# RMSNorm statistics by quarter, down-projection groups of 3 and 4, and norms moved across two stage barriers in a decoder layer

## The chip, the cores and the metric

The kernel runs on the 8 cores of one Trainium2 chip. Each core computes 2 of the 16 sequences from beginning to end; nothing is exchanged. The metric is the device time in microseconds of the slowest core.

## The reference

One decoder layer on x of 16 × 2048 × 1024 float32, and a last norm. In short:

```
x = x + 0.5 * swiglu(rmsnorm(x, g1), gate1, up1, down1)      # D = 1024, D_FF = 2816
h = rmsnorm(x, g_mix)
proj = h @ w_in                                              # 1024 -> 3072
A = 4 differential-attention heads (causal, over all 2048 keys)
B = 8 dilated sliding-window heads, windows/strides (128,1), (512,4), (2048,16)
x = x + concat(A, B) @ w_out
x = x + 0.5 * swiglu(rmsnorm(x, g2), gate2, up2, down2)
y = rmsnorm(x, g_fin)
rmsnorm(x, g) = x / sqrt(mean(x*x) + 1e-5) * g ; swiglu = (silu(x@gate) * (x@up)) @ down
```

## The kernel before, in words

A sequence is held in SBUF as `x_sb`: 16 tiles (NT) of 128 tokens by 1024 features, float32. Its stages run one after the other, for each of the two sequences: FFN1 norm, FFN1, mix norm, differential attention and its output projection, dilated attention and its output projection, FFN2 norm, FFN2, final norm.

A norm that feeds matmuls is `norm_to_hT` (L344). It loads the gain (one transfer on SyncE's queue, L336), calls `row_stats_all` (L338), and then goes over the 16 tiles. `row_stats_all` is 16 Square activations on ScalarE (L297; each squares a tile into `junk` and adds up its rows into a column of `ss`), one Sqrt over all 16 columns, and one reciprocal on VectorE (L342) that leaves `rstd`. For each tile VectorE multiplies by `rstd` and gain into one of two buffers `hb` (L308), TensorE transposes its eight 128×128 blocks into PSUM bank 6 or 7 (L353), and the bank is copied into `hT`, by ScalarE for even tiles (L356) and by VectorE for odd ones (L315). `final_norm` (L762) has no transposes: VectorE writes the tile into one of two output buffers (in `acc`) and SyncE's queue sends it to HBM.

`ffn` (L361) goes over 22 chunks of 128 hidden features. Per chunk and quarter of the tokens: 8 gate and 8 up matmuls of 128×512 (PSUM banks 0 to 3), Silu on ScalarE, a product on VectorE into a ring `aT` of 8 chunks. The weights of a chunk are three transfers that GpSimd issues, into rings of 3 (gate, up) and 6 (down) chunks. After every fourth chunk, and after the last, comes a down-projection group: for 16 tiles and 2 halves, one matmul per chunk of the group is summed up in PSUM bank 4 or 5, and VectorE adds 0.5 times the bank to `x_sb` (L308, `scalar_tensor_tensor`). So the groups have 4, 4, 4, 4, 4 and 2 chunks.

The order on each engine is the order of emission; nothing is reordered. `Sched.op` (L74) derives the waits from declared reads and writes. `Sched.barrier` (L64) notes the last operation of every engine and the last DMA of every semaphore key; the next operation that each engine has after it waits for them all, and `run_engine` (L149) writes that as one wait instruction after the other, leaving out those that this engine has made before:

```
            for d in o.deps:
                sem, val = d.signal
                k = id(sem)
                if waited.get(k, 0) < val:
                    eng.wait_ge(sem, val)
```

A barrier stands after FFN1, after the mix norm, after the first output projection, and after the second one. Behind the mix norm's barrier SyncE loads the positions, VectorE and ScalarE compute rotation tables in turn (`rope_tables`, each step waits for the one before), and GpSimd issues four `w_out` loads and then the first `w_in` loads. SBUF region `U16` is shared: the FFN's weight rings lie where the attention's `mixT`, which the output projection reads, lies.

Of the kernel before, what the change touches and what calls it, by code (L numbers as in the profile page):

```python
# [14 lines left out]
D = 1024  # L15
# [5 lines left out]
G = 4  # L21
LAMBDA_INIT = 0.8 - 0.6 * math.exp(-0.3 * 0)
# [145 lines left out]
def build_nc(nseq=2, stages=("ffn1", "attn", "ffn2"), debug_out=None):  # L168
# [88 lines left out]
    R_ss = Res("ss")  # L257
    R_rstd = Res("rstd")
# [79 lines left out]
    def row_stats_all():  # L338
        for t in range(NT):
            act(junk[:], x_sb[:, t, :], AF.Square, [R_x[t]], [R_junk, R_ss], accum_out=ss[:, t:t + 1])  # L340
        act(rstd[:], ss[:], AF.Sqrt, [R_ss, R_eps], [R_rstd], bias=epsc[:], scale=1.0 / D)
        SC.op("dve", lambda e: e.reciprocal(out=rstd[:], in_=rstd[:]), [R_rstd], [R_rstd])  # L342

    def norm_to_hT(g_ap):  # L344
        load_gain(g_ap)
        row_stats_all()
        for t in range(NT):
            k = t % 2
            stt("dve", hb[:, k, :], x_sb[:, t, :], rstd[:, t:t + 1], gain[:], ALU.mult, ALU.mult,
                [R_x[t], R_rstd, R_gain], [R_hb[k]])  # L350
            for dc in range(8):
                SC.op("pe", lambda e, o=pt[k][:, dc * 128:(dc + 1) * 128], i=hb[:, k, dc * 128:(dc + 1) * 128]:
                      e.transpose(o, i, ident[:]), [R_hb[k], R_ident], [R_pt[k]])  # L353
            src = pt[k].rearrange("p (c t) -> p c t", c=8)
            if t % 2 == 0:
                SC.op("act", lambda e, o=hT[:, :, t * 128:(t + 1) * 128], i=src: e.copy(out=o, in_=i),  # L356
                      [R_pt[k]], [R_hT[t]])
            else:
                tcopy("dve", hT[:, :, t * 128:(t + 1) * 128], src, [R_pt[k]], [R_hT[t]])

    def ffn(wg_d, wu_d, wd_d):  # L361
# [4 lines left out]
        for c in range(NCH):  # L366
# [18 lines left out]
            if (c + 1) % G == 0 or c == NCH - 1:  # L385
                c0 = (c // G) * G
                grp = list(range(c0, c + 1))
# [361 lines left out]
    def attention(s_, which):  # L749
        norm_to_hT(g_mix)  # L750
# [6 lines left out]
        if "B" in which:  # L757
            dil_stage()
            out_proj(512)
        SC.barrier()  # L760

    def final_norm(s):  # L762
        load_gain(g_fin)
        row_stats_all()
        for t in range(NT):
            k = t % 2
            stt("dve", ostage[:, k, :], x_sb[:, t, :], rstd[:, t:t + 1], gain[:], ALU.mult, ALU.mult,
                [R_x[t], R_rstd, R_gain], [R_ostage[k]])
# [3 lines left out]
    for s in range(nseq):  # L772
        for t in range(NT):
            dma("sp", x_sb[:, t, :], x_in[s, t * 128:(t + 1) * 128, :], [], [R_x[t]], ("x", t))
        if "ffn1" in stages:
            norm_to_hT(g_ffn1)
            ffn(w1g, w1u, w1d)
            SC.barrier()
# [6 lines left out]
        if "ffn2" in stages:  # L785
            norm_to_hT(g_ffn2)
# [88 lines left out]
```

How the kernel before makes its waits and increments, by code:

```python
    def run_engine(self, e, eng, final_waits=None):  # L149
        waited = {}
        for o in self.ops[e]:
            for d in o.deps:
                sem, val = d.signal
                k = id(sem)
                if waited.get(k, 0) < val:
                    eng.wait_ge(sem, val)
                    waited[k] = val
            ins = o.fn(eng)
            if o.need_inc:
                sem, _ = o.signal
                ins.then_inc(sem, 16 if o.dma_key is not None else 1)
        if final_waits:
            for sem, val in final_waits:
                if waited.get(id(sem), 0) < val:
                    eng.wait_ge(sem, val)
```

## Time and profile before

| what | value |
|---|---|
| time of three runs: lowest, median, highest | 4325.0, 4445.0, 4617.3 us |
| time of the profiled execution | 4323.8 us |
| its span (first to last instruction, slowest core) | 4322.2 us |
| spans of the eight cores | 4305.7 to 4322.2 us |
| TensorE matmul busy | 3355.8 us, 15640 matmuls |
| VectorE busy / ScalarE busy / GpSimd busy | 1717.8 / 1283.3 / 677.2 us |

The profiled execution is one run, and lies next to the lowest of the three; the times of single instructions below come from it. Its own time is 1.6 us more than its span. "Busy" of TensorE is the time in which matmuls were under way. In rows of a timeline the first number is the start in us from the span's start, the second the duration; a bracket tells how long the engine had been idle before, and what ended that. "issue" there means that the engine waited for nothing that the profile shows. The times are of core 5.

### The profile page before, as it was taken

The numbers are of one execution on the slowest core, as the hardware profiler recorded it, in microseconds if no ns is written. First come the engines' busy times: TensorE is split into PE (matmuls) and PEld (weight loads), VectorE is DVE, ScalarE is ACT, GpSimd is POOL, SyncE is SP. The second block draws the span as 40 slices with busy tenths as digits, with TensorE's granted clock in tenths as the row PEclk, the third lists the DMA queues.
The fourth block names the chain that finished last, engine by engine and source line by source line (L and its number), as shares of the span: only waits on it lengthen the run. The fifth ranks groups of instructions, "written<-read, shape, count | busy, mean of one in ns | idle before, by whom it ended". The sixth has DMA issues, their size and how long they took to land.

```text
span 4322.2 us, 57072 instructions; the slowest of 8 cores (4305.7 to 4322.2 us)
## 1 busy us (share of the span) xinstructions
PE 3355.8 (78%) x15640; PEld 1404.4 (32%) x15640; DVE 1717.8 (40%) x2611; ACT 1283.3 (30%) x1959; POOL 677.2 (16%) x904
## 2 busy tenths in 40 slices
PE   1999955777587767999739999468776787599995
PEld 1444322232133323344214434132322333244442
DVE  2333444131355454433533343441314454543345
ACT  2111022636344542011221101236362546311102
POOL 0111002120043320011001100020201343101100
PEclk9999977888676668999959999678887675699998
DMA  4333202010111013233243322110101010223321
GB/s 107 37 40 40 25 6 35 1 16 1 15 11 11 6 22 37 32 38 41 46 144 42 42 30 25 20 20 1 16 1 20 6 16 1 27 35 38 44 30 78
DMA packets 256900, 129.76 MB, mean 30 GB/s; under 512 B 228816, under 2 KB 233040, under 8 KB 256592
## 3 DMA queue, kind: packets, MB, share of 16 engines
q0 software_dynamic: 243776, 86.00, 18.2%
q1 hardware_dynamic: 12816, 40.11, 2.7%
q8 instruction: 137, 2.24, 0.2%
q14 instruction: 171, 1.40, 0.1%
HBM read 195.30 MB, written 16.78 MB: 49 GB/s over the span
## 4 chain that ended last, share of the span: by engine, by line
PE 70%; issue 7%; DVE 7%; ACT 7%; DMA 6%; POOL 1%; SPq 0%; DVEq 0%; ACTq 0%; POOLq 0%
PE pall L290 65%; DMA U<-w_in 4%; PE pall L714 3%; PE pall L353 2%; ACT tmpf L295 2%; ACT U L295 2%; ACT junk L297 2%; DVE hb L308 1%; POOL U L312 1%; DVE x_sb L308 1%; DVE tmpf L312 1%; DMA y<-acc 1%; DVE acc L312 1%; DVE U L312 1%; DMA x_sb<-x 1%
## 5 line engine op out<-in xcount | busy, mean ns | idle before, releaser
L290 PE MATMUL pall<-hT,U 128*128 128x512 bf16 x6912 | 1543.7, 384 | 104.7 <-DMA U<-w_in 68.9
L290 PE MATMUL pall<-U 128*128 128x512 bf16 (+5 forms) x5424 | 1358.5, 383 | 224.5 <-DVE tmpf L312 99.1
L290 PEld LDWEIGHTS pall<-hT,U 128*128 128x128 bf16 x6912 | 680.4, 99 | 944.7 <-issue 153.6
L290 PEld LDWEIGHTS pall<-U 128*128 128x128 bf16 (+1 forms) x5424 | 429.5, 101 | 1108.9 <-issue 873.0
L295 ACT ACTIVATE tmpf<-pall 128x512 f32<-128x512 f32 (+1 forms) x384 | 243.0, 633 | 1623.3 <-PE pall L290 1623.2
L312 DVE TENSOR_TENSOR U<-tmpf,pall 128x512 bf16<-128x512 f32 x352 | 242.1, 688 | 978.8 <-PE pall L290 961.1
L308 DVE SCALAR_TENSOR_TENSOR x_sb<-pall,x_sb 128x512 f32<-128x512 f32 x768 | 529.7, 692 | 196.9 <-PE pall L290 195.4
L295 ACT ACTIVATE U<-pall 128x1024 bf16<-128x1024 f32 (+5 forms) x688 | 463.4, 697 | 299.4 <-PE pall L290 289.0
L312 DVE TENSOR_TENSOR U<-U,maskb 128x256 bf16<-128x256 bf16 (+1 forms) x496 | 143.0, 303 | 672.9 <-ACT U L295 672.0
L312 POOL TENSOR_TENSOR U<-U,maskb 128x256 bf16<-128x256 bf16 (+1 forms) x448 | 253.8, 571 | 910.9 <-ACT U L295 557.7
L353 PE MATMUL pall<-ident,hb 128*128 128x128 bf16 x768 | 96.5, 306 | 350.1 <-DVE hb L308 288.9
L290 PE MATMUL pall<-U,onesb 128*128 128x512 bf16 (+3 forms) x672 | 263.3, 400 | 71.3 <-ACT U L295 71.3
L286 POOL DMA_DIRECT2D U<-ffn_gate x88 | 78.4, 891 | 1318.4 <-PE pall L290 1221.5
L714 PE MATMUL pall<-U 128*128 128x128 bf16 (+1 forms) x816 | 189.2, 345 | 82.9 <-POOL U L312 52.7
L312 POOL TENSOR_TENSOR U<-tmpf 128x512 bf16<-128x512 f32 x128 | 170.8, 1351 | 183.2 <-DVE tmpf L312 144.3
L297 ACT ACTIVATE junk<-x_sb 128x1024 bf16<-128x1024 f32 x128 | 135.2, 1056 | 214.9 <-DVE x_sb L312 75.4
L353 PEld LDWEIGHTS pall<-ident,hb 128*128 128x128 bf16 x768 | 74.5, 138 | 373.0 <-issue 372.7
L312 DVE TENSOR_TENSOR tmpf<-junk,U 128x512 f32<-128x512 bf16 x128 | 135.9, 1062 | 106.8 <-POOL U L312 62.7
L480 ACT CAST junk<-pall 128x512 bf16<-128x512 f32 x128 | 74.8, 586 | 312.4 <-PE pall L290 255.1
L312 DVE TENSOR_TENSOR acc<-pall,acc 128x512 f32<-128x512 f32 x128 | 129.3, 1063 | 0.2 <-PE pall L714 0.2
L286 POOL DMA_DIRECT2D U<-ffn_down x88 | 49.5, 563 | 496.7 <-PE pall L290 496.7
L714 PEld LDWEIGHTS pall<-U 128*128 128x128 bf16 x816 | 62.1, 113 | 196.6 <-issue 195.3
(53 smaller groups left out, 1449.9 us busy)
## 6 DMA issues: line engine op xcount, KB each, us to landing
U<-ffn_gate POOLq DMA_DIRECT2D x88, 256.0 KB, 4.4
U<-ffn_up POOLq DMA_DIRECT2D x88, 256.0 KB, 6.3
U<-ffn_down POOLq DMA_DIRECT2D x88, 256.0 KB, 6.7
x_sb<-x SPq DMA_DIRECT2D x32, 512.0 KB, 13.2
y<-acc SPq DMA_DIRECT2D x32, 512.0 KB, 2.8
U<-w_in POOLq DMA_DIRECT2D x40, 256.0 KB, 4.5
U<-w_out POOLq DMA_DIRECT2D x16, 256.0 KB, 6.6
tmpf<-ffn_norm SPq DMA_DIRECT2D x4, 512.0 KB, 13.2
```

The lines of the kernel that those rows point to most:

```text
L286: return SC.op(eng, lambda e, o=out, i=in_: e.dma_start(out=o, in_=i), reads, writes, dma_key=key)
L290: e.matmul(o, lhsT=l, rhs=r, start=s, stop=t), reads, writes)
L295: e.activation(out=o, in_=i, func=f, bias=b, scale=s), reads, writes)
L297: e.activation(out=o, in_=i, func=f, bias=b, scale=s, accum_out=a), reads, writes)
L308: e.scalar_tensor_tensor(out=o, in0=i, scalar=s, in1=j, op0=p, op1=q), reads, writes)
L312: e.tensor_tensor(out=o, in0=i, in1=j, op=p), reads, writes)
L353: e.transpose(o, i, ident[:]), [R_hb[k], R_ident], [R_pt[k]])
L480: SC.op("act", lambda e, o=qraw[:, k, :], i=A[:]: e.copy(out=o, in_=i), [R_pb[k]], [R_qraw[k]])
L714: e.matmul(o, lhsT=l, rhs=r, start=s_, stop=False, skip_group_check=True),
```

## The change

The statistics are computed for four tiles at a time, each quarter with its own Sqrt and reciprocal over four columns, and each quarter is emitted inside the tile loop, ahead of its first tile; `ss` and `rstd` have a resource per quarter, so that a tile waits for its own quarter alone. The table `GROUP_END` sets the down groups to chunks 0–2, 3–5, 6–9, 10–13, 14–17, 18–21. The barrier between FFN1 and the mix norm is gone. The FFN2 norm is emitted ahead of the barrier that follows the second output projection, so that this barrier now stands between the FFN2 norm and FFN2.

```diff
+GROUP_END = {2: 0, 5: 3, 9: 6, 13: 10, 17: 14, 21: 18}
...
-    R_ss = Res("ss")
-    R_rstd = Res("rstd")
+    R_ss = [Res(f"ss{q}") for q in range(4)]
+    R_rstd = [Res(f"rstd{q}") for q in range(4)]
...
-    def row_stats_all():
-        for t in range(NT):
-            act(junk[:], x_sb[:, t, :], AF.Square, [R_x[t]], [R_junk, R_ss], accum_out=ss[:, t:t + 1])
-        act(rstd[:], ss[:], AF.Sqrt, [R_ss, R_eps], [R_rstd], bias=epsc[:], scale=1.0 / D)
-        SC.op("dve", lambda e: e.reciprocal(out=rstd[:], in_=rstd[:]), [R_rstd], [R_rstd])
+    def row_stats(q):
+        sl = slice(4 * q, 4 * q + 4)
+        for t in range(4 * q, 4 * q + 4):
+            act(junk[:], x_sb[:, t, :], AF.Square, [R_x[t]], [R_junk, R_ss[q]], accum_out=ss[:, t:t + 1])
+        act(rstd[:, sl], ss[:, sl], AF.Sqrt, [R_ss[q], R_eps], [R_rstd[q]], bias=epsc[:], scale=1.0 / D)
+        SC.op("dve", lambda e: e.reciprocal(out=rstd[:, sl], in_=rstd[:, sl]), [R_rstd[q]], [R_rstd[q]])
 
     def norm_to_hT(g_ap):
         load_gain(g_ap)
-        row_stats_all()
         for t in range(NT):
             k = t % 2
+            if t % 4 == 0:
+                row_stats(t // 4)
             stt("dve", hb[:, k, :], x_sb[:, t, :], rstd[:, t:t + 1], gain[:], ALU.mult, ALU.mult,
-                [R_x[t], R_rstd, R_gain], [R_hb[k]])
+                [R_x[t], R_rstd[t // 4], R_gain], [R_hb[k]])
...
-            if (c + 1) % G == 0 or c == NCH - 1:
-                c0 = (c // G) * G
-                grp = list(range(c0, c + 1))
+            if c in GROUP_END:
+                grp = list(range(GROUP_END[c], c + 1))
...
     def attention(s_, which):
-        norm_to_hT(g_mix)
         SC.barrier()
         rope_tables(s_)
...
             dil_stage()
             out_proj(512)
+        if "ffn2" in stages:
+            norm_to_hT(g_ffn2)
         SC.barrier()
 
     def final_norm(s):
         load_gain(g_fin)
-        row_stats_all()
         for t in range(NT):
             k = t % 2
+            if t % 4 == 0:
+                row_stats(t // 4)
...
         if "ffn1" in stages:
             norm_to_hT(g_ffn1)
             ffn(w1g, w1u, w1d)
-            SC.barrier()
+        if any(st in stages for st in ("attn", "attnA", "attnB")):
+            norm_to_hT(g_mix)
...
         if "ffn2" in stages:
-            norm_to_hT(g_ffn2)
+            if not any(st in stages for st in ("attn", "attnA", "attnB")):
+                norm_to_hT(g_ffn2)
             ffn(w2g, w2u, w2d)
```

ScalarE's queue, from the first norm to the mix norm, stands like this in the kernel before (`junk,ss<-x_sb` are the Squares, `rstd<-ss` the Sqrt, `COPY hT` the copies of the even tiles, `tmpf<-pall` the FFN's Silu):

```order
L297 ACTIVATE junk,ss<-x_sb 128x1024 x16
L295 ACTIVATE rstd<-ss,epsc 128x16
L356 COPY hT<-pall 128x8x128 x8
L295 ACTIVATE tmpf<-pall 128x512 x88
L297 ACTIVATE junk,ss<-x_sb 128x1024 x16
L295 ACTIVATE rstd<-ss,epsc 128x16
L356 COPY hT<-pall 128x8x128 x8
```

and like this in the changed kernel, over the first norm:

```order
L298 ACTIVATE junk,ss<-x_sb 128x1024 x4
L296 ACTIVATE rstd<-ss,epsc 128x4
L359 COPY hT<-pall 128x8x128 x2
L298 ACTIVATE junk,ss<-x_sb 128x1024 x4
L296 ACTIVATE rstd<-ss,epsc 128x4
L359 COPY hT<-pall 128x8x128 x2
L298 ACTIVATE junk,ss<-x_sb 128x1024 x4
L296 ACTIVATE rstd<-ss,epsc 128x4
L359 COPY hT<-pall 128x8x128 x2
L298 ACTIVATE junk,ss<-x_sb 128x1024 x4
L296 ACTIVATE rstd<-ss,epsc 128x4
L359 COPY hT<-pall 128x8x128 x2
```

The 16 Squares in one piece have become four pieces of four; from the second piece on they stand behind two copies of the quarter before.

SyncE's queue from the first gain load to the FFN2 norm's, with its waits (`s_` are the engines' semaphores, `d_` those of DMA keys; `tmpf` is the gain, `acc` the positions), before:

```order
L286 DMA tmpf<-ffn_norm 128x1024
L286 DMA tmpf<-mix_norm 128x1024 [waits d_25,s_dve,s_pe,s_act,d_35,d_26,d_27,d_28,d_29,d_30,d_31,d_32,d_33,d_34,d_36,d_37,d_0,d_3,d_7,d_8,d_9,d_10,d_11,d_12,d_13,d_14,d_15,d_16,d_17,d_18,d_19,d_20,d_21,d_22,d_23,d_24]
L286 DMA acc<-positions 128x512 [waits s_pe,s_act,s_dve,d_25]
L286 DMA acc<-positions 128x512
L286 DMA acc<-positions 128x512 [waits d_38,s_dve]
L286 DMA acc<-positions 128x512 [waits d_39,s_dve]
L286 DMA tmpf<-ffn_norm 128x1024 [waits s_pe,s_act,s_dve,s_pool,d_39,d_40,d_41,d_42,d_43,d_44,d_45,d_38]
```

and changed:

```order
L287 DMA tmpf<-ffn_norm 128x1024
L287 DMA tmpf<-mix_norm 128x1024 [waits d_25,s_dve]
L287 DMA acc<-positions 128x512 [waits s_pe,s_act,s_dve,d_35,d_25,d_26,d_27,d_28,d_29,d_30,d_31,d_32,d_33,d_34,d_36,d_37,d_0,d_3,d_7,d_8,d_9,d_10,d_11,d_12,d_13,d_14,d_15,d_16,d_17,d_18,d_19,d_20,d_21,d_22,d_23,d_24]
L287 DMA acc<-positions 128x512
L287 DMA acc<-positions 128x512 [waits d_38,s_dve]
L287 DMA acc<-positions 128x512 [waits d_39,s_dve]
L287 DMA tmpf<-ffn_norm 128x1024 [waits s_pe,s_act,s_dve,s_pool,d_39,d_40,d_41,d_42,d_43,d_44,d_45,d_38]
```

The long list of waits has moved from the mix norm's gain load to the first load of positions, since that is now SyncE's first operation behind the first barrier. The same happens on VectorE (from the mix norm's reciprocal to the first step of the rotation tables) and on ScalarE (from the mix norm's first Square to the first Sin of the tables).

## Rows read from the trace of the kernel before

**Rows 1.** Busy by stretch: PE, PEld, DVE, ACT, POOL (counts), clock, DMA share, GB/s.

```profile
1603.00:1660.00 57.00, 16.53 (x130) 12.73 (x131) 24.54 (x25) 28.07 (x42) 6.99 (x9) 0.52 0.43 53
```

**Rows 2.** Timeline, FFN1 end and mix norm, sequence 0: start, duration (us), engine, what.

```profile
592.36 0.69 DVE L308 SCALAR_TENSOR_TENSOR x_sb<-pall,x_sb 128x512 f32<-128x512 f32 x1 [0.25 <-PE pall L290]
...
594.36 1.06 ACT L297 ACTIVATE junk<-x_sb 128x1024 bf16<-128x1024 f32 x1 [28.01 <-issue]
...
595.17 0.33 SPq L286 DMA_DIRECT2D tmpf<-mix_norm  x1
...
612.96 1.06 ACT L297 ACTIVATE junk<-x_sb 128x1024 bf16<-128x1024 f32 x1
...
615.48 0.31 ACT L295 ACTIVATE rstd<-ss,epsc 128x16 f32<-128x16 f32 x1
...
617.12 0.25 DVE L342 RECIPROCAL rstd<-rstd 128x16 f32<-128x16 f32 x1 [24.07 <-issue]
...
654.18 0.69 DVE L315 COPY hT<-pall 128x1024 bf16<-128x1024 bf16 x1 [1.26 <-PE pall L353]
```

**Rows 3.** Timeline, second output projection's end, FFN2 norm, FFN2's start, sequence 0.

```profile
1601.99 0.69 DVE L312 TENSOR_TENSOR x_sb<-pall,x_sb 128x512 f32<-128x512 f32 x1 [0.41 <-PE pall L290]
...
1603.60 0.94 POOL L286 DMA_DIRECT2D U<-ffn_gate  x1 [48.18 <-DVE x_sb L312]
...
1625.17 0.25 DVE L342 RECIPROCAL rstd<-rstd 128x16 f32<-128x16 f32 x1 [22.49 <-ACT rstd L295]
...
1632.58 1.01 ACT L356 COPY hT<-pall 128x1024 bf16<-128x1024 bf16 x1 [3.33 <-PE pall L353]
...
1634.29 2.47 DVE L308 SCALAR_TENSOR_TENSOR hb<-x_sb,rstd,tmpf 128x1024 bf16<-128x1024 f32 x2
...
1659.44 10.88 PE L290 MATMUL pall<-hT,U 128*128 128x512 bf16 x42
...
1659.75 0.69 DVE L315 COPY hT<-pall 128x1024 bf16<-128x1024 bf16 x1 [1.26 <-PE pall L353]
```

**Rows 4.** Timeline, first norm of sequence 0: gain transfer's issue, first normalization.

```profile
47.34 4.06 SPq L286 DMA_DIRECT2D tmpf<-ffn_norm  x1
...
70.36 2.48 DVE L308 SCALAR_TENSOR_TENSOR hb<-x_sb,rstd,tmpf 128x1024 bf16<-128x1024 f32 x2 [0.17 <-DVE rstd L342]
```

**Rows 5.** DMA issues of 40 to 70 us, gain row: KB, us from issue to landing.

```profile
tmpf<-ffn_norm SPq DMA_DIRECT2D x1, 512.0 KB, 20.7
```

**Rows 6.** DMA issues, first gate weights at 118.0, 3740.9 and 1603.6 us.

```profile
U<-ffn_gate POOLq DMA_DIRECT2D x1, 256.0 KB, 4.6
...
U<-ffn_gate POOLq DMA_DIRECT2D x1, 256.0 KB, 6.7
...
U<-ffn_gate POOLq DMA_DIRECT2D x1, 256.0 KB, 9.5
```

**Rows 7.** Timeline, VectorE adds of a two-chunk group, then of a four-chunk group.

```profile
570.49 1.36 DVE L308 SCALAR_TENSOR_TENSOR x_sb<-pall,x_sb 128x512 f32<-128x512 f32 x2 [0.17 <-PE pall L290]
...
588.94 1.36 DVE L308 SCALAR_TENSOR_TENSOR x_sb<-pall,x_sb 128x512 f32<-128x512 f32 x2 [0.17 <-PE pall L290]
...
1719.46 0.69 DVE L308 SCALAR_TENSOR_TENSOR x_sb<-pall,x_sb 128x512 f32<-128x512 f32 x1 [0.41 <-PE pall L290]
...
1747.02 0.69 DVE L308 SCALAR_TENSOR_TENSOR x_sb<-pall,x_sb 128x512 f32<-128x512 f32 x1 [0.41 <-PE pall L290]
```

**Rows 8.** Timeline, final norm of sequence 0: last add, first output tile.

```profile
2146.44 0.69 DVE L308 SCALAR_TENSOR_TENSOR x_sb<-pall,x_sb 128x512 f32<-128x512 f32 x1 [0.17 <-PE pall L290]
...
2150.65 2.48 DVE L308 SCALAR_TENSOR_TENSOR acc<-x_sb,rstd,tmpf 128x1024 f32<-128x1024 f32 x2 [0.18 <-DVE rstd L342]
```

**Rows 9.** Groups by line, ScalarE's table loads: busy us, mean ns, idle before.

```profile
L295 ACT ACT_TABLE_LOAD x16 | 20.5, 1283 | 65.5 <-DVE lams L327 34.8 <-DVE tmpf L304 17.7 <-PE pall L290 12.3
```

**Rows 10.** Timeline, after mix norm: positions' issue, first rotation matmul.

```profile
655.01 4.47 SPq L286 DMA_DIRECT2D acc<-positions  x3
...
688.59 0.58 PE L290 MATMUL pall<-junk,perm 128*128 128x512 bf16 x1 [10.29 <-ACT junk L480]
```

More of the change, by code:

```diff
@@ L763, in final_norm @@
         load_gain(g_fin)
-        row_stats_all()
         for t in range(NT):
             k = t % 2
+            if t % 4 == 0:
+                row_stats(t // 4)
             stt("dve", ostage[:, k, :], x_sb[:, t, :], rstd[:, t:t + 1], gain[:], ALU.mult, ALU.mult,
-                [R_x[t], R_rstd, R_gain], [R_ostage[k]])
+                [R_x[t], R_rstd[t // 4], R_gain], [R_ostage[k]])
             out_dmas.append(dma("sp", y_out[s, t * 128:(t + 1) * 128, :], ostage[:, k, :], [R_ostage[k]], [],
```

## The prediction

> **What bounds the kernel now.** I read the busy time by stretch first, then the timeline of the norms, the adds of the down groups, the transfers and the table loads. TensorE is busy for 78% of the span, so what can be won lies where it is not, and the norms are such places. In the FFN2 norm of sequence 0 it works 16.5 of 57 us, VectorE 24.5 and ScalarE 28.1 [rows 1]: no engine is the bound, they take turns. The reader is to see two halves there. First 16 Squares in a row, one every (612.96 − 594.36)/15 = 1.24 us, then Sqrt and reciprocal [rows 2]. Then the tile loop, from the reciprocal at 1625.17 to the end of the last copy at 1660.44, 35.3 us [rows 3], in which VectorE multiplies two tiles, waits for the transposes and copies one. Whatever of a norm lies beside a matmul stage is won; whatever is moved inside the tile loop is not hidden, since TensorE's next matmuls stand behind the transposes of all 16 tiles.
>
> **The statistics inside the loop.** This is the term that decides. In the changed order ScalarE has 4 Squares, Sqrt, 2 copies, 4 Squares and so on. The Squares of quarter 1 stand behind the copy of tile 2, and that copy waits for tile 2's transposes. In the loop of before this copy ends at 1632.58 + 1.01 = 1633.59, and VectorE starts tile 4 at 1634.29 [rows 3]. Now 4 Squares (4 × 1.24 = 4.96), the Sqrt (0.31, [rows 2]) and the reciprocal (0.25, [rows 3]) come in between, with three handovers of about 0.2 (the reciprocal's to the multiply is 0.17, [rows 4]): tile 4 starts at about 1633.59 + 5.86 = 1639.45, 5.2 us late. That comes three times per norm, 15.5 us; the Squares of quarter 0 alone can be ahead of the loop. So a loop costs 35.3 + 15.5 = 50.8 us from its first reciprocal. At least the 4.96 us of Squares less the 0.7 of slack, 4.3, must show; 6.0 would need half a microsecond for each handover: 13 to 18 us per norm.
>
> **FFN1 norm.** The Squares were hidden before: they follow x from HBM. Now only quarter 0 is needed early, but the first multiply also needs the gain, which SyncE issues behind all 16 tiles of x, at 47.34, and which lands 20.7 us later, at 68.0 [rows 4, 5]. Before, the first multiply started at 70.36 [rows 4]. So it comes at 68.2, 2.2 us sooner, and the loop is 15.5 longer: **+13.3 us**. Were the gain there at once, tile 0 could start some 17 us sooner, but it is not, and the change leaves its place in the queue alone.
>
> **Mix norm.** Before, from the last add's end (592.36 + 0.69 = 593.05) to the last copy's end (654.87) it is 61.8 us [rows 2]. Now the Squares of quarter 0 run under the last down group, the gain has long landed, and VectorE's reciprocal stands right behind its last add: 0.1 + 50.8 = 50.9, so 10.9 less. But the barrier's waits were paid in this stretch: ScalarE's first Square came 1.3 us after the last add, SyncE's gain load 2.1, and the reciprocal started 617.12 − 615.79 = 1.3 after the Sqrt [rows 2]. These lists are not removed but move to the first operation behind the mix norm, as the order of SyncE's queue shows: the load of positions, which came 0.14 us after the last copy (655.01, [rows 10]), then VectorE's first table step, then ScalarE's first Sin. These are one chain, and TensorE waits at its end: 10.3 us for a cast that stands behind the last Sin [rows 10]. So 2.0 + 1.2 + 1.2 = 4.4 come back. TensorE's and GpSimd's own lists are covered by that wait. **−6.5 us** (−10.9 if the lists cost nothing there).
>
> **FFN2 norm.** The last add of the output projection ends at 1602.68, FFN2's first matmul comes at 1659.44 [rows 3]. Now the loop's last copy ends at 1602.68 + 0.1 + 50.8 = 1653.6. But the barrier has moved behind it, and with it the first weights, which before were issued at 1603.60 under the Squares, 0.9 us after the barrier's last operation [rows 3]: issue at 1654.5, landing 4.6 to 9.5 us later. I take the middle row, 6.7 [rows 6]; the shortest is of the steady state with no burst of nine loads, the longest had the gain load beside it. TensorE's own list of ten waits adds about 0.8, priced like GpSimd's 0.9. First matmul at 1662.0: **+2.6 us** (+0.5 to +5.4). Here the cover that hid the loads is gone, and it eats the 5.9 us that the hidden quarter wins.
>
> **Final norm.** The Squares already ran beside the last down group; from the last add's end (2147.13) to the first output tile it took 3.5 us: a Square, a table load, Sqrt, reciprocal [rows 8]. Now quarter 0 is done long before, and reciprocal and handovers remain, 0.5 us. The later quarters' reciprocals fall into VectorE's waits for the output buffers. **−3.0 us**.
>
> **Down groups.** Work is the same: 22 × 32 matmuls and 6 × 32 adds per FFN. A group is paced by its two PSUM banks, which are filled, read and refilled in turn: a pair of adds takes (588.94 − 570.49)/12 = 1.54 us with two chunks and (1747.02 − 1719.46)/14 = 1.97 with four [rows 7]. That is 0.216 per matmul of each bank's sum, so three chunks should take 1.755. Then before 5 × 16 × 1.97 + 16 × 1.54 = 182.2 us per FFN, after 4 × 16 × 1.97 + 2 × 16 × 1.755 = 182.2. **0 us**. The bounds are three chunks at the pace of two (2 × 16 × 0.215 = −6.9 per FFN, −28 over four) or of four (+28). The weights' ring of six down chunks frees its slots as early as before: groups end at 2, 5, 9, 13, 17 and the load of chunk c needs c − 6 done, never later than chunk c − 3.
>
> **Table loads.** The Trainium skill, "ScalarE: Activation LUTs", section "Table sets: the hidden batching unit", says to batch activations by table set, and speaks against Sqrts strewn among other functions; it names copy among the fillers of every set, but not the Square. By that rule each switch would cost what its section "What ACT_TABLE_LOAD costs" gives, about 2.66 us with its drain; an estimate from this page is 2 × 3 × 6 switches, some 96 us. What follows does not need the page. The trace has 16 loads of 1.28 us [rows 9]. Counting the changes of function in the program (Exp at the start; Sqrt, Silu, Sqrt, Sin, Exp with Ln, Sqrt, Silu, Sqrt in sequence 0; in sequence 1 the same less the first Sqrt) gives 1 + 8 + 7 = 16, so no Square and no copy ever brought one, and the new Sqrts bring none. By this count the term is 0.
>
> **Sum.** Per sequence 13.3 − 6.5 + 2.6 − 3.0 = +6.4; I take both sequences alike, so +12.8 us: 4323.8 + 12.8 = 4336.6, **4337 us**, +0.3%. This stands against the profiled execution, at the low end of the three runs. Their median is 4445, 2.8% above it, more than all terms together; the same program can come out there again (4445 + 13 = 4458).
>
> **Rivals.**
> - *The statistics overlap as meant.* If ScalarE's Squares of later quarters cost the loop nothing, 6 × 15.5 = 93 us go: 4244. The order speaks against it: in a queue that runs in order they stand behind copies that wait. 3%.
> - *Three-chunk groups run at the pace of VectorE.* Two chunks at 1.54 are near two adds of 0.69 with their handovers; if three are too, −28: 4309. Against it: two matmuls more per bank already cost their full time between two and four chunks. 12%.
> - *Three-chunk groups at four chunks' pace*, +28: 4365. 5%.
> - *Slower: table reloads.* If the Square or the copy needed another set than Sqrt, each of three later quarters in six norms would load twice on the path: 36 × 1.28 = 46 us, 4383. It decides from the first load seen between a copy and a Square. The count above is against it. 4%.
> - *Slower: the weights behind the moved barrier.* If gate weights land after 9.5 us and the stall per quarter is 6.0, it is 2 × 2.8 + 6 × 2.5 = +21: 4358. 8%.
>
> **How the numbers follow.** The forecast (4337) has 65%, the rivals 32%, something not thought of 3%. The terms' own bounds give 4315 to 4358; the low end 4300 takes in the case of faster three-chunk groups; the high end 4460 takes in the slower cases and a run at the median shown before. All cases lie within 2% (86 us), about what a measurement of this kernel can tell from no change; for a scatter like that of the runs shown, and for what I missed, I leave 7% faster and 7% slower, 86% within.
>
> **What would show it.** In the changed profile: 16 table loads again; in each tile loop three gaps of VectorE of about 5 us before tiles 4, 8 and 12, ended by ScalarE; last add to last copy about 51 us at the mix norm; the positions' load 2 us after the mix norm; FFN2's first matmul waiting for its gate weights, some 8 us after the last copy; first output tile 0.5 us after the last add; a pair of adds at 1.75 us in the groups of three. It is wrong if the Squares of later quarters lie beside the copies of earlier ones, if more than 16 table loads are there, or if an FFN's length changed by more than a few us.

## The result and the profile after

The changed kernel takes 4394.7 us, the median of 10 runs (4347.82 to 4761.62); the kernel before, run beside it, 4426.2 (10 runs, 4324.18 to 4709.0). Some executions of either kernel run with the TensorE clock of one die lower and take 80 to 410 us longer, 6 of the 10 of before and 5 of the 10 of the changed kernel, which is why the medians stand the other way round; so the two are compared without them, and so is every ratio below. That ratio is **1.0066 (95% interval 1.005 to 1.0082)**: the change costs 0.7% or about 28 us. The forecast was 12.8 us. The profiled execution took 4350.43 us against 4323.8. First two of its cores:

```profile
core 1: 4348.9 us, clock 0.843
core 5: 4346.6 us, clock 0.844
```

One core of each die, at the clock that before had on them (0.844 and 0.845): the difference is work and waits, not clock.

**Where it went.** From the timelines of all eight cores of both kernels I took the times of a few events of VectorE (the last add and the last copy of a norm, the first product of an FFN, the first and last output tile) and of the output projections' ends. The table has the mean of eight cores of each stage, in us, as sequence 0 / sequence 1. A norm between two stages is the same on all cores to within 0.5. The stages that wait for transfers (the first norm of a sequence, attention, FFN2's first weights, the output tiles of sequence 0) differ by up to 6 from the shortest to the longest core, so that a mean of eight is good to about 1.

| stage | before | after | measured | forecast |
|---|---|---|---|---|
| start (sequence 1: last output tile of sequence 0) to the last copy of the FFN1 norm | 104.7 / 67.9 | 117.9 / 81.1 | +13.2 / +13.2 | +13.3 |
| FFN1, last copy to last add | 487.9 / 486.2 | 486.3 / 487.2 | −1.6 / +1.0 | 0 |
| mix norm, last add to last copy | 61.8 / 60.7 | 49.3 / 49.7 | −12.6 / −11.1 | −10.9 |
| to the end of the first output projection | 512.1 / 509.6 | 516.9 / 514.7 | +4.8 / +5.0 | +4.4 |
| to the end of the second | 431.8 / 430.0 | 433.4 / 432.2 | +1.6 / +2.2 | 0 |
| FFN2 norm and wait for its first product | 62.2 / 62.2 | 65.2 / 64.7 | +3.0 / +2.5 | +2.6 |
| FFN2, first product to last add | 481.9 / 481.6 | 481.0 / 480.7 | −0.9 / −0.9 | 0 |
| last add to first output tile | 3.5 / 3.5 | 0.3 / 0.3 | −3.2 / −3.2 | −3.0 |
| first to last output tile | 32.2 / 31.7 | 42.3 / 33.3 | **+10.1** / +1.7 | 0 |
| sum | 4311.4 | 4336.2 | +24.8 | +12.8 |

All terms that were forecast with a size came within 2 us. What was missed stands in rows forecast as 0: the output tiles (+11.8) and the way to the second output projection (+3.8); the FFNs give 2.4 back.

**The tile loop.** These rows are VectorE's and ScalarE's part of the mix norm in the timeline of after, sequence 0, core 1 ([rows 2] has that of before):

```profile
603.31 0.69 DVE L309 SCALAR_TENSOR_TENSOR x_sb<-pall,x_sb 128x512 f32<-128x512 f32 x1 [0.18 <-PE pall L291]
603.92 0.17 DVE L344 RECIPROCAL rstd<-rstd 128x4 f32<-128x4 f32 x1
...
610.85 1.01 ACT L359 COPY hT<-pall 128x1024 bf16<-128x1024 bf16 x1 [3.43 <-PE pall L356]
611.76 1.06 ACT L298 ACTIVATE junk<-x_sb 128x1024 bf16<-128x1024 f32 x1
...
617.12 0.18 DVE L344 RECIPROCAL rstd<-rstd 128x4 f32<-128x4 f32 x1 [4.47 <-ACT rstd L296]
617.40 2.48 DVE L309 SCALAR_TENSOR_TENSOR hb<-x_sb,rstd,tmpf 128x1024 bf16<-128x1024 f32 x2
...
630.65 0.18 DVE L344 RECIPROCAL rstd<-rstd 128x4 f32<-128x4 f32 x1 [4.47 <-ACT rstd L296]
...
644.19 0.18 DVE L344 RECIPROCAL rstd<-rstd 128x4 f32<-128x4 f32 x1 [4.48 <-ACT rstd L296]
...
652.56 0.69 DVE L316 COPY hT<-pall 128x1024 bf16<-128x1024 bf16 x1 [1.26 <-PE pall L356]
```

Read it from ScalarE's side: its copy of tile 2 (610.85) has to wait for tile 2's transposes, and the four Squares of the next quarter stand right behind it, so VectorE has nothing to multiply for 4.47 us. The first reciprocal, on the other hand, stands right behind the last add (603.31 + 0.69 = 604.00; the trace has the reciprocal start 0.08 before that). Last add to last copy is 653.25 − 604.00 = 49.3 us where 50.9 was forecast.

**The FFN2 norm's end**, timeline of after, sequence 0, core 1, and its gate transfer in the view of DMA issues (KB, us to landing):

```profile
1654.51 0.69 DVE L316 COPY hT<-pall 128x1024 bf16<-128x1024 bf16 x1 [1.27 <-PE pall L356]
1655.64 0.33 SPq L287 DMA_DIRECT2D tmpf<-final_norm  x1
1656.17 0.94 POOL L287 DMA_DIRECT2D U<-ffn_gate  x1 [97.67 <-DVE hT L316]
...
1664.41 15.87 PE L291 MATMUL pall<-hT,U 128*128 128x512 bf16 x62 [10.00 <-DMA U<-ffn_gate]
```

```profile
U<-ffn_gate POOLq DMA_DIRECT2D x1, 256.0 KB, 7.8
```

TensorE stands for 10.0 us, and it names the gate weights. They are issued 1.0 us after the last copy's end and land 7.8 us later; before, they were issued 0.9 us behind the output projection's last add, ahead of the norm [rows 3]. Compare [rows 1] with the same norm in after on the same core, 5 (PE, PEld, DVE, ACT, POOL busy with counts, clock, DMA share, GB/s). TensorE and VectorE work about as long as before. ScalarE has 5.6 us less, the Squares and the Sqrt of quarter 0. GpSimd's 6.99 us, the issues of the weights, are gone from the norm, and no transfer is under way in it. No engine is the bound in after either.

```profile
1603.50:1654.00 50.50, 16.18 (x128) 12.39 (x128) 25.79 (x29) 22.46 (x35) 0.00 (x0) 0.52 0.00 0
```

**The first norm**, after, core 1. The reciprocal of quarter 0 comes at 49.59, some 20 us before that of before, which stood right ahead of the multiply at 70.36 [rows 4]. Yet this wins only 1.6 and 2.2 us (mean of the cores, sequence 0 and 1), since the multiply now waits for the gain. The second fence is ScalarE's table loads in the view of groups: 16 again, as in [rows 9].

```profile
46.70 4.28 SPq L287 DMA_DIRECT2D tmpf<-ffn_norm  x1
...
49.59 0.18 DVE L344 RECIPROCAL rstd<-rstd 128x4 f32<-128x4 f32 x1 [10.23 <-ACT rstd L296]
68.25 2.48 DVE L309 SCALAR_TENSOR_TENSOR hb<-x_sb,rstd,tmpf 128x1024 bf16<-128x1024 f32 x2 [18.48 <-DMA tmpf<-ffn_norm]
```

```profile
L296 ACT ACT_TABLE_LOAD x16 | 20.5, 1283 | 98.3 <-PE pall L291 35.4 <-DVE lams L328 35.1 <-DVE tmpf L305 14.2
```

**The output tiles of sequence 0**, where most of the missed time is. First comes the timeline of after (core 1), then the transfers issued in this stretch, then the same two of before (core 5):

```profile
2151.28 0.55 POOL L287 DMA_DIRECT2D U<-ffn_down  x1 [29.73 <-PE pall L291]
...
2151.95 0.88 POOL L287 DMA_DIRECT2D U<-ffn_gate  x1
...
2152.44 2.48 DVE L309 SCALAR_TENSOR_TENSOR acc<-x_sb,rstd,tmpf 128x1024 f32<-128x1024 f32 x2 [0.18 <-DVE rstd L344]
...
2155.97 0.60 POOL L287 DMA_DIRECT2D U<-ffn_down  x1
2163.06 2.48 DVE L309 SCALAR_TENSOR_TENSOR acc<-x_sb,rstd,tmpf 128x1024 f32<-128x1024 f32 x2 [8.15 <-DMA y<-acc]
...
2173.13 2.50 DVE L309 SCALAR_TENSOR_TENSOR acc<-x_sb,rstd,tmpf 128x1024 f32<-128x1024 f32 x2 [7.50 <-DMA y<-acc]
```

```profile
y<-acc SPq DMA_DIRECT2D x6, 512.0 KB, 8.6
U<-ffn_down POOLq DMA_DIRECT2D x3, 256.0 KB, 11.8
U<-ffn_gate POOLq DMA_DIRECT2D x2, 256.0 KB, 10.5
```

```profile
2120.28 0.88 POOL L286 DMA_DIRECT2D U<-ffn_gate  x1 [69.53 <-PE pall L290]
...
2126.58 0.93 POOL L286 DMA_DIRECT2D U<-ffn_up  x1
2146.68 0.56 POOL L286 DMA_DIRECT2D U<-ffn_down  x1 [19.17 <-PE pall L290]
...
2154.86 2.50 DVE L308 SCALAR_TENSOR_TENSOR acc<-x_sb,rstd,tmpf 128x1024 f32<-128x1024 f32 x2 [1.73 <-DMA y<-acc]
```

```profile
y<-acc SPq DMA_DIRECT2D x12, 512.0 KB, 2.7
```

Look at GpSimd first (in after there are three down, two gate and two up loads in this stretch). The next sequence's loads (gate, up, down of chunk 0 and so on) stand in its queue in order. A ring slot holds every sixth chunk, so the down load of chunk 0 takes slot 0, in which chunk 18 of this sequence lies. Before, the last group was 20 and 21, chunk 18 was used up in the group 16 to 19, and eight loads went out at 2120 to 2127, under the matmuls; only that of chunk 2 waited. Now the last group is 18 to 21. The load of chunk 0 waits 29.73 us for its end, six more stand behind it, and all seven meet the first output stores. A store then takes 8.6 us instead of 2.7, and VectorE has only two output buffers: it waits twice for about 8 us instead of 1.7.

**The wait lists**, core 5 after, behind the mix norm. The last copy is issued at 652.80; against [rows 10] the positions' load, the first table step and the Sin's table load are all late:

```profile
652.80 0.69 DVE L316 COPY hT<-pall 128x1024 bf16<-128x1024 bf16 x1 [1.26 <-PE pall L356]
655.70 17.42 SPq L287 DMA_DIRECT2D acc<-positions  x4
...
662.98 0.49 DVE L303 TENSOR_SCALAR tmpf<-acc,invf 128x512 f32<-128x512 int32 x1 [9.48 <-issue]
...
668.00 1.28 ACT L296 ACT_TABLE_LOAD   x1 [15.29 <-issue]
```

From the last copy's end (653.49) the three are 2.2, 9.5 and 14.5 us; before they were 0.1, 3.7 and 7.7. Not all of this is lists: on this core the positions also took 5.9 us to land, and 3.4 before, and over cores and sequences that time scatters from 3.1 to 6.7 before and from 3.5 to 6.0 in after. What is the same on all eight cores of sequence 0 is 2.1 us more ahead of the issue, and a first table step 1.4 us behind the landing instead of 0.17; from that step to the table load it is 5.0 us instead of 3.9 to 4.3. The first rotation matmul, at the end of this chain, comes 39.8 and 38.0 us after the last copy (sequence 0 and 1, mean of the cores), and came 34.3 and 34.5 before. The profile writes "issue" for a list, since no semaphore event ends it.

### The profile page after: what moved, and what is told of

The parts are those of the page before. It is cut to its first block, busy times and chain, and to the rows that moved or that the text cites. A ratio compares the mean times of both kernels' runs of the same rounds, so it can differ in the third digit from the quotient of the medians.

```text
span 4348.9 us, 57066 instructions; the slowest of 8 cores (4330.5 to 4348.9 us)
## 1 busy us (share of the span) xinstructions
PE 3368.6 (77%) x15640; PEld 1404.9 (32%) x15640; DVE 1718.6 (40%) x2635; ACT 1288.3 (30%) x1983; POOL 678.4 (16%) x904
## 4 chain that ended last, share of the span: by engine, by line
PE 71%; issue 8%; DMA 7%; DVE 6%; ACT 6%; POOL 1%; SPq 0%; DVEq 0%; ACTq 0%; POOLq 0%
PE pall L291 65%; DMA U<-w_in 3%; PE pall L716 3%; ACT tmpf L296 2%; ACT U L296 2%; PE pall L356 2%; DVE hb L309 2%; ACT junk L298 1%; POOL U L313 1%; DMA y<-acc 1%; DVE tmpf L313 1%; DMA tmpf<-ffn_norm 1%; DVE U L313 1%; DVE acc L313 1%; PE pall L664 1%
## 5 line engine op out<-in xcount | busy, mean ns | idle before, releaser
L309 DVE SCALAR_TENSOR_TENSOR hb<-x_sb,rstd,tmpf 128x1024 bf16<-128x1024 f32 x96 | 118.8, 1279 | 38.7 <-DMA tmpf<-ffn_norm 36.1
L359 ACT COPY hT<-pall 128x1024 bf16<-128x1024 bf16 x48 | 48.6, 1012 | 270.3 <-PE pall L356 270.3
## 6 DMA issues: line engine op xcount, KB each, us to landing
tmpf<-ffn_norm SPq DMA_DIRECT2D x4, 512.0 KB, 12.1
```

Source lines behind the costliest of these rows:

```text
L309: e.scalar_tensor_tensor(out=o, in0=i, scalar=s, in1=j, op0=p, op1=q), reads, writes)
```

## The experiments

The ratios are against the kernel before, run on the same chip. "Stages" are means of eight cores, worked out as in the table above; where a stage is named without a sequence, sequence 0 stands first.

**Groups back.** The changed kernel with the old groups:

```diff
-GROUP_END = {2: 0, 5: 3, 9: 6, 13: 10, 17: 14, 21: 18}
+GROUP_END = {3: 0, 7: 4, 11: 8, 15: 12, 19: 16, 21: 20}
```

> The changed kernel with the down groups of before (4,4,4,4,4,2 chunks). Theory, burst of weights: with chunk 18 in the last group, the next sequence's first down load waits for that group's end, and six gate, up and down loads behind it in GpSimd's queue are issued together with the first output tiles; these took 8.6 us to land instead of 2.7. With the old groups the burst is over before the outputs begin: from the first to the last output tile of sequence 0 the time falls from 42.3 (mean of the cores) to about 33 us, the other stages stay, and the span falls by 9 to 12 us, to about 4338. Rival, pace of the groups: the groups of three and four themselves cost the time; then the two FFNs of a sequence get shorter or longer by several us, and the output stretch stays at 42.

Measured: 1.0035 (1.002 to 1.005), profiled 4341.14 us. The output tiles of sequence 0 are back at 33.2 us (after 42.3), and a store lands after 2.8 us. The four FFNs, in their order, move by +1.3, 0.0, −0.8 and +1.7 against after. So the regrouping costs through the output tiles, and not in the FFNs (what these 0.8 to 1.7 us are stands in the last section).

**Groups only.** The kernel before with the new groups and nothing else:

```diff
+GROUP_END = {2: 0, 5: 3, 9: 6, 13: 10, 17: 14, 21: 18}
-            if (c + 1) % G == 0 or c == NCH - 1:
-                c0 = (c // G) * G
-                grp = list(range(c0, c + 1))
+            if c in GROUP_END:
+                grp = list(range(GROUP_END[c], c + 1))
```

> The kernel before with the new group table alone. Theory, burst of weights: the output stretch of sequence 0 grows from 32.2 to 38 to 44 us (the first output tile comes 3.5 us later here than in the changed kernel, so some of the burst is past), all else stays, span 4322 + 6 to 12 = 4328 to 4334. Rival, pace of the groups: FFN stages change by more than 2 us each and the output stretch stays near 32. Nothing at all (4322) would say that the burst needs the other edits.

Measured: 1.0036 (1.0018 to 1.0053). Sequence 0's output tiles take 39.7 us against 32.2, +7.5, and those of sequence 1 +0.1: the cost needs a next sequence whose weights are to be loaded. The rest of the +15.7 us of the sum lies in the attention (+1.0, −0.3, +4.3, +0.4), in FFN2 of sequence 0 (+1.6) and FFN1 of sequence 1 (+1.1; see the last section). The +4.3, on the way to the first output projection of sequence 1, is more than the scatter of a mean, and no edit of this run touches that stage: its cause is open, and it is a warning for what small differences of this stage are taken to show. By the ratios both experiments give about the same: half of what the change costs is the regrouping.

**Groups 3, 4, 4, 4, 4, 3.** A last group of three, 19 to 21, so that chunk 18 is done one group earlier:

```diff
-GROUP_END = {2: 0, 5: 3, 9: 6, 13: 10, 17: 14, 21: 18}
+GROUP_END = {2: 0, 6: 3, 10: 7, 14: 11, 18: 15, 21: 19}
```

> The changed kernel with groups of 3, 4, 4, 4, 4 and 3 chunks, so that the last group holds chunks 19 to 21 and no longer chunk 18, whose slot the next sequence's first down load takes. Theory, burst of weights: the slot decides, not the sizes: the output stretch of sequence 0 falls from 42.3 to about 33 us as in the run with the old groups, FFN stages stay within 1 us, span about 4339. Rival, any last group of three or four chunks delays the outputs (its adds end later beside them): stays at 40 or above.

Measured: 4345.37 us in the profiled run; there is no ratio for it. The output tiles take 38.4 us, so 4.0 of 9.1 us are gone, where I had expected all of them to go. The timeline of its slowest core has the reason, and it is the same mechanism:

```profile
2158.05 0.56 POOL L287 DMA_DIRECT2D U<-ffn_down  x1 [24.20 <-PE pall L291]
2158.72 0.88 POOL L287 DMA_DIRECT2D U<-ffn_gate  x1
...
2168.97 2.66 DVE L309 SCALAR_TENSOR_TENSOR acc<-x_sb,rstd,tmpf 128x1024 f32<-128x1024 f32 x2 [7.50 <-DMA y<-acc]
2173.15 2.58 DVE L309 SCALAR_TENSOR_TENSOR acc<-x_sb,rstd,tmpf 128x1024 f32<-128x1024 f32 x2 [1.44 <-DMA y<-acc]
```

Now it is the load of chunk 1 that waits, for chunk 19, and three loads are behind it instead of six. VectorE waits once for 7.5 us instead of twice. What the stores lose goes by how many loads come out at the group's end: one, four, seven loads give 33.2, 38.4, 42.3 us.

**Statistics first.** The changed kernel, but with the Squares and Sqrts of all four quarters ahead of the loop; only the reciprocals stay at the quarters:

```diff
+        for q in range(4):
+            row_stats(q)
...
-                row_stats(t // 4)
+                row_recip(t // 4)
```

> The changed kernel with the Squares and Sqrts of all four quarters emitted ahead of the tile loop in the six norms with transposes; the reciprocals stay at each quarter. Theory, order of ScalarE's queue: the three stalls of about 4.9 us in each loop are the Squares behind the copies; they go, and at the mix and FFN2 norms the Squares lie beside the adds before them. Norm from last add to last copy 49.4 to about 36 us, FFN1 norm's loop 49.7 to about 36, six times 13.5 = 81 us less: span about 4268. Rival, cost per quarter: the stall comes with each quarter's own Sqrt, reciprocal and waits wherever the Squares are; then loops stay above 45 us and the span above 4325.

Measured: **0.987 (0.9848 to 0.9893)**, profiled 4265.31 us, 83 us less than after in the stages' sum. The loop's rows (mix norm, sequence 0, slowest core):

```profile
597.25 0.17 DVE L347 RECIPROCAL rstd<-rstd 128x4 f32<-128x4 f32 x1
597.52 2.48 DVE L309 SCALAR_TENSOR_TENSOR hb<-x_sb,rstd,tmpf 128x1024 bf16<-128x1024 f32 x2
...
606.22 0.17 DVE L347 RECIPROCAL rstd<-rstd 128x4 f32<-128x4 f32 x1
```

The reciprocals are 8.97 us apart, not 13.54, and no gap is before them. A norm from last add to last copy takes 35.6 to 36.0 us, the FFN1 loop 35.7. So the stall is the Squares' place in ScalarE's queue, and all four quarters' Squares fit under the last group of adds (or the output projection): the rival by which the statistics overlap as meant (forecast 4244 for it) describes this kernel, not the changed one.

**Barrier back.** The changed kernel with the second barrier ahead of the FFN2 norm again:

```diff
+        SC.barrier()
...
-        SC.barrier()
```

> The changed kernel with the barrier again between the second output projection and the FFN2 norm. Theory, weights behind the barrier: from the last copy to FFN2's first product the time falls from 15.3 to 4.4 us, as before, since the first weights load under the norm; the norm itself pays the barrier, four Squares, a table load and Sqrt in the open, about 49.6 + 8 = 57.5 us. Net per sequence 3 us less, span about 4343. Rival, TensorE starts slowly there for another reason (its clock after the idle time): the stretch stays above 10 us although the weights are there.

Measured, in a single run: 4345.89 us. The weights go out during the norm, as before, and VectorE's first product comes 4.7 us after the last copy (after: 15.6 and 15.1); but the Squares of quarter 0 are no longer hidden and the norm takes 57.3 us (after 49.6). Together 62.0 against 65.2 and 64.7. The move of the barrier is therefore a loss of 3 us a sequence: it hides 7.7 us of Squares and uncovers 10.6 of weights. The way to the second output projection is 2.5 and 1.7 us shorter as well, which is the next experiment's subject.

**Short wait lists.** The barrier leaves out DMAs that some later operation has already waited for:

```diff
-        allp = lasts + list(dl.values())
+        allp = lasts + [o for o in dl.values() if not o.seen]
...
+            d.seen = True
```

> The changed kernel with barriers that leave out every DMA which an engine has already waited for (its last operation then covers it); the SyncE list at the positions' load falls from 39 names to 5. Theory, price of the lists: the stretch from the mix norm's last copy to the end of the first output projection falls by about 4.4 us, from 516.9 and 514.7 (mean of the cores, two sequences) to 512.5 and 510.5, which is what the kernel before had; the stretch from FFN2 norm's last copy to FFN2's first product falls by 1 to 1.5 us. Together 10 to 12 us, span about 4338. Rival, the lists cost nothing and the 5 us come from something else in that stretch (clock, transfers): it stays at 517 and 515.

Measured: 1.0042 (1.0029 to 1.0056), profiled 4342.91 us. On core 5, sequence 0:

```profile
653.82 0.69 DVE L318 COPY hT<-pall 128x1024 bf16<-128x1024 bf16 x1 [1.27 <-PE pall L358]
654.69 13.22 SPq L289 DMA_DIRECT2D acc<-positions  x4
658.57 0.79 DVE L305 TENSOR_SCALAR tmpf<-acc,invf 128x512 f32<-128x512 int32 x1 [4.05 <-DMA acc<-positions]
662.79 1.28 ACT L298 ACT_TABLE_LOAD   x1 [9.07 <-DVE tmpf L307]
```

From the copy's end it is 0.2, 4.1 and 8.3 us again, and VectorE now waits for the transfer, not for its list. The first rotation matmul comes 34.7 and 35.4 us after the last copy (mean of the cores, sequence 0 and 1), 5.1 and 2.7 sooner than in after. So the lists are worth some 4 us a sequence where they stand on the positions' chain, as forecast. The first output projection is 6.0 and 1.2 us sooner, while FFN2 of sequence 0 takes 2.6 more, and the stages' sum falls by 5.7 us only, where I had expected 10 to 12.

**Gain late.** The FFN2 gain's load waits until the second output projection has begun:

```diff
-            norm_to_hT(g_ffn2)
+            norm_to_hT(g_ffn2, after=[R_x[0]])
```

> The changed kernel with the FFN2 norm's gain load made to wait for the second output projection's first tile. Theory, gain load in the way: in the changed kernel this load of 512 KB is issued together with the loads at the dilated stage's start, and the first w_in lands 12.2 instead of 10.0 us after its issue; with it gone from there, the stretch from the first to the second output projection's end falls by 2 us, from 433.4 and 432.2 to about 431.2 and 430.2, all else the same: span 4 us less. Rival, noise or the early statistics: it stays.

Measured: 1.0048 (1.0033 to 1.0063). The way to the second projection is 1.4 and 2.3 us shorter than in after, but that to the first 1.4 longer in both, so that the sum moves by 0.7 us only, where I had expected 4. These are the dilated stage's first two w_in loads on core 1 of sequence 0, KB and us to landing, before and after:

```profile
U<-w_in POOLq DMA_DIRECT2D x2, 256.0 KB, 9.3
```

```profile
U<-w_in POOLq DMA_DIRECT2D x2, 256.0 KB, 12.2
```

One core does not settle it: with barrier back, which has no gain load there either, they took 7.5 us, but in this experiment, without one too, 11.4. All eight cores do, in sequence 1. There the first w_in load lands after 8.1 to 9.9 us in after and 7.0 to 7.4 in gain late, and TensorE's first matmul comes 13.1 us behind the first output projection in after, 11.0 in gain late and 11.2 before. In sequence 0 it is 14.7, 13.1 and 12.1. So the gain's 512 KB do cost the weights time: all of what this wait grew by in sequence 1, and 1.5 of 2.6 us in sequence 0.

**Repaired.** Old groups, statistics of all quarters ahead of the loop, short lists, gain late, and for FFN2 the statistics ahead of the barrier but the loop behind it, so that the weights go out before the tiles:

```diff
+            norm_stats(g_ffn2, after=[R_x[0]])
...
+        if "ffn2" in stages:
+            norm_loop()
```

> All repairs together: down groups of before; Squares and Sqrts of all quarters ahead of the loop; at the FFN2 norm they stand ahead of the barrier and the tile loop behind it, so that the first weights load under the loop; late gain load; short lists. If the terms add up, mean of the cores: norm from last add to last copy 36 at the mix and 37.5 at the FFN2 norm, 4.5 us to FFN2's first product, 33 us for the output tiles, first output projection's stretch 512 and 510, second's 431: span about 4225, 97 us or 2.2% below the kernel before. Rival, terms that cover each other: above 4245.

Measured: two runs of 4232.31 and 4234.05 us, too few for an interval, beside 4326 to 4332 of before, so about 2.2% less. The stages below are from cores 0 to 3 of the profiled run, at a granted clock of 0.852 to 0.854; their spans are 4215.6 to 4231.1 us, where 4225 was expected. FFN2 norm and wait for its first product take 41.8 us (37.9 + 3.9) instead of 65.2: both the hidden Squares and the early weights.

**Gain first.** As repaired, and in the FFN1 norm the gain is loaded ahead of x; the Squares of two quarters stand ahead of the loop, those of quarter q + 1 at quarter q:

```diff
+            load_gain(g_ffn1)
...
-            norm_stats(g_ffn1)
-            norm_loop()
+            row_stats(0)
+            row_stats(1)
+            norm_loop(ahead=True)
```

> The repaired kernel with the FFN1 norm's gain loaded ahead of x, and there the Squares of one quarter ahead of the loop's quarter. Theory, gain as the gate of the first norm: the first tile can start when quarter 0 is there, at about 52 instead of 68 us, and the loop then follows x from HBM: last copy at about 95 instead of 104 us, and as much in sequence 1: 14 to 18 us less than the repaired kernel, span about 4210. Rival, ScalarE's queue again: the Squares ahead wait for x and hold up the copies, so that less than 6 us is won in all.

Measured: **0.9713 (0.9701 to 0.9726)**, profiled 4205.74 us. The first multiply on its slowest core:

```profile
54.34 0.18 DVE L349 RECIPROCAL rstd<-rstd 128x4 f32<-128x4 f32 x1 [11.60 <-ACT rstd L298]
54.70 2.48 DVE L311 SCALAR_TENSOR_TENSOR hb<-x_sb,rstd,tmpf 128x1024 bf16<-128x1024 f32 x2 [0.17 <-DVE rstd L349]
```

It comes 14 us sooner than in after (68.25), and what it waits for is now x by way of ScalarE, not the gain, which lands after 6.2 us instead of 21.5. The loop stays at 35.9 and 36.8 us though Squares stand in it: one quarter ahead, the tiles no longer wait for them. Per sequence the first tile comes 15.6 and 16.2 us sooner than in the repaired kernel; I had expected about that for both together. This kernel and the next one are the fastest of the study: 2.9% below the kernel before.

**w_in first.** As gain first, but the w_out loads stand behind the first projections' weights in both attention stages:

```diff
-            wout_dma(0)
...
+            if g == 0:
+                wout_dma(0)
```

> The repaired kernel with the gain first, and the four w_out loads of each attention stage issued behind the first group of projections instead of ahead of w_in. At the dilated stage TensorE's first matmul waits 14 us for w_in, four loads of 256 KB ahead of it in the queue; with w_in first it should wait 7 to 8: 6 us less between the two output projections, per sequence. At the differential stage the tables are the later wait, so nothing is won there. Together 12 us less, span about 4192. Rival, the landing is bound by issue and not by the queue of transfers: under 4 us in all.

Measured: 0.9711 (0.9696 to 0.9725), no different from gain first; the stages' sum falls by 3.7 us, where I had expected 12. What was aimed at came: w_in lands after 4.8 and TensorE waits 6.37 instead of 13.53 us for it (core 1, the dilated stage; the first row is of gain first):

```profile
1138.33 6.43 PE L293 MATMUL pall<-hT,U 128*128 128x512 bf16 x16 [13.53 <-DMA U<-w_in]
```

```profile
1140.98 4.92 PE L293 MATMUL pall<-hT,U 128*128 128x512 bf16 x16 [6.37 <-DMA U<-w_in]
```

and the second output projection comes 4.0 and 5.6 us sooner. But the first comes 4.0 and 2.5 later, and that takes most of it back. What in the first stage gives it back I have not shown; the w_out issues now stand on GpSimd among its work of the rotation, which would fit.

## Why the prediction was right and wrong

- **The loop (+15.5 a norm): right in its mechanism, 1 us too high.** The stall per quarter is 13.54 − 8.69 = 4.85 us, where 8.69 is four tiles' time in the loop of before (two tiles take 4.35); forecast 5.2. The bound of 4.3 to 6.0 held. A loop took 49.3 to 50.2 us, forecast 50.8. Statistics first shows that the Squares' place is the cause, since moving them takes the stall away.
- **FFN1 norm: right.** +13.24 and +13.23, forecast +13.3. The gain gates the first tile, as foreseen (it lands after 21.5 us); before, the reciprocal did. Gain first shows that the 17 us called possible there are 14 to 16.
- **Mix norm: right.** −7.7 and −6.0 with what comes back behind it, forecast −6.5. The price of the lists, forecast 4.4, shows on the way to the first rotation matmul, which grew by 5.5 and 3.5 us; short lists take 5.1 and 2.7 of it away. The stage's +4.8 and +5.0 agree, but prove less, since groups only has +4.3 there without any list moved. The norm itself won 12.6 and 11.1 instead of 10.9.
- **FFN2 norm: right.** +3.0 and +2.5, forecast +2.6; the gate weights landed after 7.8 us instead of 6.7, against which the loop was shorter, and the first matmul came 0.4 us behind the landing where 0.8 was priced for TensorE's list. Barrier back gives the same from the other side.
- **Final norm: right up to its first tile, −3.2 for −3.0**, but not all of it reaches the last tile. From the last add to the last output tile it is 35.7 us before and 33.5 with groups back in sequence 0, and 35.2 and 33.6 in sequence 1: 2.2 and 1.6 us won. In the changed kernel itself nearly nothing of it is left in sequence 0, where the stores wait for the loads: 42.6 us, and 43.2 in groups only, which has no earlier first tile.
- **Down groups, 0: the step that failed.** Their pace was right: the 32 adds of a three-chunk group take 27.85 us, between 24.95 of two and 31.07 of four (1.75 a pair, forecast 1.755), and all adds of FFN2 in sequence 0 take 180.3 us before and 180.0 after. What failed is the sentence "The weights' ring of six down chunks frees its slots as early as before". I had compared chunk c with chunk c − 6 of the same FFN, and there it holds. The ring runs on into the next sequence's FFN: its chunk 0 takes the slot of this one's chunk 18, which the new last group holds to the end. That is +10.1 us at the output tiles of sequence 0, of which groups back takes 9.1 away; the whole miss in the stages is 24.8 − 12.8 = 12.0 us. It is also where "I take both sequences alike" was wrong: the last sequence has no next.
- **The move of the gain load, 0: not priced.** The order shows it ahead of the dilated stage; I followed SyncE's queue, where it costs nothing, and not the w_in loads beside it. +3.8 us in the stage. The wait for w_in at its start grew by 2.6 and 1.9 us, and gain late takes back 1.5 and 2.1 of that.
- **Table loads: right.** 16 again. The trace has Sqrt, copy and Square in turn without a load between them. So the rule of the Trainium skill, "ScalarE: Activation LUTs", section "Table sets: the hidden batching unit", to batch activation calls by set, has nothing to gain here.
- **The rivals.** None of them came. The stall at 6.0 with late weights was the nearest (4358), but with measured 4.85 and 7.8 us its mechanism was not there; the loss beyond the forecast has another source, which no rival had.
- **The number.** 4337 was set against a profiled execution at the low end of the runs shown, and the step from it, +0.3%, was less than half of the measured +0.7%. That it stood below the median shown while a loss was forecast comes from the scatter of the runs, as the text said; the direction and the verdict (within 2%) were right, the size was not.

## What to carry to other kernels

Splitting a statistic per quarter pays only if its parts stand in their engine's queue where that engine waits anyway: ahead of the loop or one quarter ahead, not behind the copy that itself waits for the loop. Whoever changes when a buffer of a ring is released has to follow the ring past the end of its loop to whatever fills it next, and ask which transfers those loads will meet. And a barrier that is moved past a stage takes with it every prefetch behind it; split the stage, and put the barrier between the part that reads old data and the part that can hide the loads.

## What the runs showed of the hardware

- **Seven weight loads beside a store.** 512 KB from SyncE's queue land in 2.7 us alone and in 8.6 us when seven 256 KB loads from GpSimd's queue are under way. In the stretch the two moved 2.40 MB and 1.84 MB, but the loads took 66.0% of the DMA engines' time and the stores 27.0%:

```profile
q0 software_dynamic: 4592, 1.84, 66.0%
q1 hardware_dynamic: 649, 2.40, 27.0%
```

  Nearly all packets of the first are under 512 B (4272 of the 5241 of both). So a load that is small in bytes can hold a larger transfer up. Whether it is the small packets that do it was not tried apart.
- **Waiting lists have a price.** With everything long done, the barrier's list took SyncE 2.2 us where a short one took 0.2, VectorE's first step came 1.4 us behind the landing it needs where it came 0.24 behind it with the short list, and "issue" is all that the profile writes for it.
- **A pause of 0.35 us in a down group.** In every build some FFNs take 31.42 us for the 32 adds of a four-chunk group and others 31.07 (three chunks 28.20 or 27.85, two chunks 24.95 or 24.6). In the kernel before it is FFN1 of sequence 0 that is slow, in after FFN1 of sequence 1, in groups only and short lists FFN2 of sequence 0 too. The pace is the same, 1.97 us a pair; there is one pause of 0.35 us, at the same add in each group of that FFN. Four or five groups of it are most of the −1.6, +1.0, +1.3 and +1.7 us by which FFN stages moved. The instructions are the same, and the cause is open.
- **A slower end.** In after, groups back, statistics first and gain late, the last 16 output tiles take 33.3 us instead of 31.7; in the builds with short lists they take 31.7 again. In after, the fifth and sixth store land in 3.2 to 3.8 us and not in 2.7. What runs beside them there wasn't tried apart.
